# PEER gate phase: three weighted one-hot rows of eight made in one VectorE operation each, straight from the iota row

## The reference, cut to what matters

```python
idx = (i1 * PEER_KEYS + i2)          # per token 8 heads x 16 experts, i1 and i2 in 0..127
g = softmax(gv, axis=-1)
u = expert_u[idx_blk]                # block of tokens
a = g_blk * gelu(einsum('tkd,td->tk', u, x_blk))
out = einsum('tk,tkd->td', a, expert_v[idx_blk])
```

## Time and profile before

| what | us |
|---|---|
| three executions | 3479.38, 3453.22, 3475.49 |
| median | 3475.49 |
| span of the profiled execution, first to last instruction | 3451.3 |
| the time nearest above that span, taken as its own | 3453.22 |
| gate phase, first one-hot compare to the last store's issue | 2224.5 to 2494.6 |
| gate phase, to the first instruction of phase B | 2526 |

### The profile page before, as it was taken

One profiled execution on the slowest core, in us unless ns is written; L12 is line 12 of the kernel. 1 busy time (PEld: TensorE's weight loads), 2 busy tenths in 40 slices (PEclk: granted clock), 3 DMA queues, 4 the chain that ended last, 5 costly groups with the idle time before them and its releaser, 6 DMA issues. The chain is left out here.

```text
span 3451.3 us, 42749 instructions
## 1 busy us (share of the span) xinstructions
PE 3047.1 (88%) x16184; PEld 2375.8 (69%) x16184; DVE 2172.9 (63%) x4563; ACT 1137.0 (33%) x1747; POOL 1466.4 (42%) x1108
## 2 busy tenths in 40 slices
PE   5996879697879979999999999876749999999996
PEld 4885768587768868787777777654437666676665
DVE  4244774415436758897878876687647666655456
ACT  3213551304221134333333333387612222222222
POOL 3100002300210048876777677687724444424532
PEclk9996799899989989999999999998879999999998
DMA  5333012421422289999999999899999999989992
GB/s 179 114 101 122 1 67 87 140 71 53 140 80 74 62 300 395 395 410 379 410 410 410 403 410 412 345 388 397 406 345 360 372 375 377 351 311 368 381 347 100
DMA packets 371629, 936.06 MB, mean 271 GB/s; under 512 B 32849, under 2 KB 134873, under 8 KB 370401
## 3 DMA queue, kind: packets, MB, share of 16 engines
q0 software_dynamic: 147456, 536.94, 39.8%
q1 hardware_dynamic: 223968, 396.39, 32.1%
HBM read 825.53 MB, written 107.67 MB: 270 GB/s over the span
## 5 line engine op out<-in xcount | busy, mean ns | idle before, releaser
L1654 POOL DMA_INDIRECT ex_ring<-in_expert_v,ex_idxT_sb x405 | 462.8, 1143 | 512.2 <-PE ex_ps_v L1679 224.5
L1654 POOL DMA_INDIRECT ex_ring<-in_expert_u,ex_idx_sb x307 | 399.1, 1300 | 190.3 <-issue 87.5
L110 PE MATMUL eo_ps<-eo_v_hi_sb,aT_late_hi 128*128 128x512 f32 x1024 | 409.1, 400 | 42.2 <-DVE aT_late_lo L2281 42.2
L1663 DVE CUSTOM_DVE_ANT_0 ex_ring<-ex_ring,ex_xg 128x1024 f32<-128x1024 f32 x307 | 368.4, 1221 | 94.3 <-DMA ex_ring<-in_expert_u,ex_idx_sb 92.9
L110 PE MATMUL ex_ps_h<-aT_late_hi,ex_uT_hi_sb 128*128 128x512 f32 x1024 | 413.1, 403 | 1.9 <-ACT ex_uT_lo_sb L1810 1.1
L112 PE MATMUL ex_ps_h<-aT_late_hi,ex_uT_lo_sb 128*128 128x512 f32 x1024 | 402.1, 393 | 0.0
L111 PE MATMUL eo_ps<-eo_v_lo_sb,aT_late_hi 128*128 128x512 f32 x1024 | 401.5, 392 | 0.0
L111 PE MATMUL ex_ps_h<-aT_late_lo,ex_uT_hi_sb 128*128 128x512 f32 x1024 | 400.4, 391 | 0.0
L112 PE MATMUL eo_ps<-eo_v_hi_sb,aT_late_lo 128*128 128x512 f32 x1024 | 400.3, 391 | 0.0
L2289 DVE TENSOR_TENSOR eo_acc<-eo_acc,eo_ps 128x1024 f32<-128x1024 f32 x124 | 151.3, 1221 | 273.2 <-PE eo_ps L112 273.1
L1679 PE MATMUL ex_ps_v<-ex_ring,ex_w_sb 128*32 128x512 f32 x1620 | 233.2, 629 | 82.0 <-DMA ex_ring<-in_expert_v,ex_idxT_sb 66.8
(11 more groups left out here) (368 smaller groups left out, 6424.9 us busy)
## 6 DMA issues: line engine op xcount, KB each, us to landing
ex_u_raw<-in_expert_u SPq DMA_DIRECT2D x128, 512.0 KB, 8.3
eo_v_raw<-in_expert_v SPq DMA_DIRECT2D x124, 512.0 KB, 8.2
act_d<-ex_act SPq DMA_DIRECT2D x128, 256.0 KB, 6.1
gate_d<-ex_gate SPq DMA_DIRECT2D x8, 4096.0 KB, 15.6
eo_g_raw<-gate_d SPq DMA_DIRECT2D x64, 512.0 KB, 8.1
eo_a_raw<-act_d SPq DMA_DIRECT2D x124, 256.0 KB, 6.5
pin_raw<-in_w_in SPq DMA_DIRECT2D x20, 512.0 KB, 4.3
n_row<-h_d SPq DMA_DIRECT2D x16, 512.0 KB, 5.9
```

The source lines that it names most:

```text
L110: pe.matmul(ps, l_hi, r_hi, start=first, stop=False)
L1654: pool.indirect_dma_start(rows(n), None, table, bass.IndirectOffsetOnAxis(at, 0)).then_inc(ring_in[slot[n]], 16)
L1663: dve.tensor_tensor_reduce(out=u, in0=u, in1=xg[:, j, :], scale=1.0, scalar=0.0, op0=ALU.mult, op1=ALU.add, accum_out=hg[:, j, k:k + 1]).t ...
```

## The change

The compare for hot2 makes only the 5 rows that ScalarE multiplies. The other 3 weighted rows no longer come from hot2: for each of them one VectorE operation compares the iota row with i2 and multiplies by the weight, both taken from `cols` as one value for each partition, and writes `ex_hw` directly. `hot_done` is now raised by the shorter compare, a new semaphore `hot1_done` by hot1, and TensorE waits for it too. VectorE's wait for its own `hot_done` before the rest is dropped. What is computed stays the same.

```diff
                                     t = slice(n * HOT_GROUP, (n + 1) * HOT_GROUP)
-                                    for hot, q in ((hot1, 1), (hot2, 2)):
-                                        last = dve.tensor_tensor(hot_rows(hot, n), iota[:].unsqueeze(1).broadcast_to([P, HOT_GROUP, P]),
-                                                                 cols[:, q, t].unsqueeze(2).broadcast_to([P, HOT_GROUP, P]), ALU.is_equal)
-                                    last.then_inc(hot_done, 1)
+                                    dve.tensor_tensor(hot_rows(hot1, n), iota[:].unsqueeze(1).broadcast_to([P, HOT_GROUP, P]),
+                                                      cols[:, 1, t].unsqueeze(2).broadcast_to([P, HOT_GROUP, P]), ALU.is_equal).then_inc(hot1_done, 1)
+                                    t = slice(n * HOT_GROUP, n * HOT_GROUP + HOT_BY_ACT)
+                                    dve.tensor_tensor(hot_rows(hot2, n)[:, 0:HOT_BY_ACT, :], iota[:].unsqueeze(1).broadcast_to([P, HOT_BY_ACT, P]),
+                                                      cols[:, 2, t].unsqueeze(2).broadcast_to([P, HOT_BY_ACT, P]), ALU.is_equal).then_inc(hot_done, 1)
 
                                 def weighted_rest(n):
-                                    dve.wait_ge(hot_done, n + 1)
                                     if n >= HW_SLOTS:
                                         dve.wait_ge(gate_mm, 2 * (n - HW_SLOTS + 1))
-                                    t = slice(n * HOT_GROUP + HOT_BY_ACT, (n + 1) * HOT_GROUP)
-                                    rest = hot2[:, n % HOT_SLOTS, HOT_BY_ACT * P:].bitcast(F32).rearrange("p (x t) -> p x t", t=P)
-                                    dve.tensor_tensor(hw[:, n % HW_SLOTS, HOT_BY_ACT:HOT_GROUP, :], rest,
-                                                      cols[:, 0, t].unsqueeze(2).broadcast_to([P, HOT_GROUP - HOT_BY_ACT, P]), ALU.mult).then_inc(hw_done_v, 1)
+                                    for x in range(HOT_BY_ACT, HOT_GROUP):
+                                        t = n * HOT_GROUP + x
+                                        last = dve.tensor_scalar(hw[:, n % HW_SLOTS, x, :], iota[:], cols[:, 2, t:t + 1], cols[:, 0, t:t + 1],
+                                                                 ALU.is_equal, ALU.mult)
+                                    last.then_inc(hw_done_v, 1)
...
                                     pe.wait_ge(hw_done_v, n + 1)
+                                    pe.wait_ge(hot1_done, n + 1)
```

More of the change, by code:

```diff
@@ L1604, in expert_stages @@
             hidden_done, av_done, avT_done, w_done, sum_g = sem("ex_hidden"), sem("ex_av"), sem("ex_avT"), sem("ex_w"), sem("ex_sum_g")
+            hot1_done = sem("ex_hot1")
             hot_done, gate_mm, gate_out = sem("ex_hot"), sem("ex_gate_mm"), sem("ex_gate_out")
```

## The result

The changed kernel takes 3497.71 us in the median of 4 runs (3495.84 to 3516.8), the kernel before 3471.76 us in 4 runs of the same comparison (3453.22 to 3479.38). The ratio is 1.0086, with a 95% interval of 1.0047 to 1.0125: under the 1% named ahead of the prediction, but clear of 1. Forecast were 3471.5 us and a range of 3448 to 3484.

The account below looks back on a forecast made before the run. DMA queues were taken to bound the gate phase, save its first 35 us where VectorE is full. VectorE's -0.6 us wasn't added to -4 us from faster gather issue; 3475.49 less 4 gave 3471.5 us, range 3448 to 3484.

Parts of the forecast that it names:

- Terms 1 to 3: VectorE in the gate phase: shorter compare, product gone, three scalar operations added; -0.06 us a group, -0.6 us on the path.
- the long stretch: Gate phase from 2260 to 2495 us, DMA share 1.01 at 405 GB/s, taken as bound by the DMA queues.
- Term 4: Semaphore waits of VectorE, TensorE and ScalarE in the gate phase: changing them brings nothing but in the first group.
- Term 5: First 35 us of the gate phase: new boundaries let GpSimd start 3 more gathers, -4 us.
- The main claim: Gate phase from 2260 to 2495 us: DMA queues are full, so time taken from VectorE there only makes it wait longer.
- The point it gave for GpSimd to take the lead: Gate phase from 2260 to 2495 us: at 1.54 us for a gather GpSimd takes the lead over the queues.
- signs of being wrong: Gate phase: mean gather over 1.54 us, DMA share below 0.95, certain TensorE waits, or length changed by over 10 us.
- two-port lock: Rival, gate phase: the new scalar operations hold gathers repeatedly while they run, +24 to +56 us; chance 0.07.
- GpSimd's rate also limits the long stretch: Rival, gate phase from 2260 to 2495 us: issue and queues both near their end, -6 us more, 3465; chance 0.07.
- From the trace to the median: Whole kernel: -4 us from the profiled execution is taken off the 3475.49 us median, giving 3471.5 us.

Follow-up runs that it names:

- three_products: Changed kernel with three two-input operations of 128 columns, without pointers, in place of the three scalar operations: ratio 0.9983 to the kernel before, phase 295.1 us.
- narrow_and_product: Changed kernel with a two-input product of 384 columns in place of the three scalar operations, 640-column compare kept: ratio 0.9987 to the kernel before, phase 298.4 us.
- tiny_copies: Kernel before with three one-column copies from SBUF added for each group ahead of the product: ratio 1.0043 to the kernel before, phase 317.4 us.
- iota_in_psum_before: Kernel before with the iota row of both compares read from PSUM instead of SBUF: ratio 0.9975 to the kernel before, phase 290.9 us.

## Why the prediction was wrong, point by point

*Terms 1 to 3, VectorE's own time: right.* The compare took 825 ns for 819 forecast, the scalar operations 349 in the median for 352. VectorE's busy time in the long stretch fell (171.7 us for 174.6, in a stretch 31 us longer), and TensorE waited for its part of `ex_hw` once, 5.4 us (6.1 before).

*Term 4, the waits: right.* The new semaphore alone changed nothing (0.9996), and putting the dropped wait back didn't cure the change.

*Term 5, what GpSimd gets: this is the step that failed.* It laid out the new boundaries and let a gather take any of them that came 1.24 us behind the last, "one per 1.59 us". The layout was fitted to the kernel before, where every operation of the phase has two inputs in SBUF, and it was carried over to a kernel with operations of another kind. The runs show that these spoil the boundaries behind them. In 30.4 us from the first gather on, 12 start, one per 2.60 us, where the sum had 19 to 20, one per 1.59, and 17 started before; in the long stretch a gather takes 1.61 us. So the term is +31 us in the phase, not -4. Where the kinds stay as they were, the term came about as forecast: `three_products` starts 20 gathers in 30.4 us, one per 1.57 (its steps in the same layout give 1.58), `narrow_and_product` 19, one per 1.65, and their phases are 6.6 and 3.3 us shorter, for the -4 us forecast. For `narrow_and_product` the layout gives 1.97 with its limit of 1.24 us and 1.65 with 1.20: a boundary 0.73 + 0.47 us behind the last is still taken.

*The main claim, that the queues bound the long stretch and cover everything: right in the main for the kernel before, but with less room than the text used.* The point it gave for GpSimd to take the lead was 1.54 us for a gather in the mean. The change went over it (1.61) and lost its 31 us. But there is no sharp point: `tiny_copies` lost 16 us at 1.51, and the kernel before gained 11 when its mean fell from 1.37 to 1.00. The text had the price of the far side and the threshold, but gave the case 0.07, and under half of that to a loss over 35 us. Three of its own signs of being wrong came: a mean over 1.54 us, a DMA share under 0.95 (0.94), and a phase changed by more than 10 us.

*The rival "two-port lock": right in what is hit and near in size (+24 to +56 us forecast, +31 in the phase), wrong in how.* It expected gathers to be held in the scalar operations. They aren't: of the 10 that start beside these in the change 7 take 0.94 to 1.01 us, and of the 70 gathers held 53 are let in where the scalar operations begin or a dot ends. What is lost are the boundaries between two-input operations that follow. So it is partly luck that its 3499 us lies beside the measured 3497.7. The one gather of the earlier trace rows that I held against the rival started inside scalar operations, and the next, at 1685.08, found VectorE idle, so it couldn't show this.

The Trainium skill's "SBUF — State Buffer", section "Who interferes with whom", has operations in a two-port mode and GpSimd exclude each other for a whole instruction, and "VectorE: DVE Perf Modes" of the Trainium skill, section "Why PSUM operands drop a tier", says that an operand in PSUM keeps an operation out of that mode. The sign agrees: 317.4 us with copies from SBUF, 303.3 from PSUM. The place doesn't agree: the gathers lose their time in the two-input operations behind, and whether the one-column copies run in a two-port mode no run shows. Pointer operands cost most here (358.7 and 362.6 us).

*"GpSimd's rate also limits the long stretch": refused at 0.07 with "-6 more", and true of the kernel before.* With the compares' holds gone (`iota_in_psum_before`) the long stretch ran at 416 GB/s instead of 405. The DMA share of 1.01 that stood against it is no proof of a full queue: it reads 1.02 there.

*From the trace to the median.* The times of the kernel before, 3453 to 3479 in one comparison and 3441 to 3461 in another, make +0.9% (26 us) hard to see in three executions. The range, though, held no room for a case that had its price worked out, +24 to +56 us.

**What stays open.** Why a gather misses the boundaries between two-input operations once operations with one SBUF input or a pointer are mixed in. The runs show which kinds do it, that it isn't the place where the gather starts, and where gathers are let in. What passes between the two engines isn't in the trace. Nor is it settled why one operation of 384 columns with pointers costs 4 us and three of 128 cost 30, nor how much of a pointer's cost is its length.

## What to carry to other kernels

Where GpSimd issues the transfers that bound a stage, ask of every VectorE operation beside it not only how long it takes but what it reads: one with two SBUF inputs holds a gather until it ends, and a few tiny ones with a single SBUF input or a pointer operand can hold gathers over the whole chain behind them, at 16 to 61 us in a phase of 302. Read GpSimd's mean time for a gather against the room it has (here 1.37 of 1.54 us) before calling the queues the bound, and don't take the room for a threshold: a shorter mean gained time and a longer one lost it, on both sides of 1.37 us. Where PSUM has room, try a small constant operand that all compares share from there: here it took the hold away and 11 us off the phase, more than any saving of VectorE's own time.

## What the runs showed of the hardware that I had not expected

Three copies of one column for each group, 141 ns each and off every path, cost 16 us in a phase of 302 (317.4 us), and a one-column operation with pointer operands 61 us (362.6 us), by way of GpSimd's gathers. The same operations with two SBUF inputs or with their input in PSUM cost nothing to 1.6 us. A pointer operand also makes a one-column operation longer, 213 ns for 154 with two inputs, and 264 for 142 with one input and two pointers.
